# Opening of w_in turned tile by tile, expert choice by rank, and constant products at the last experts

## The chip, the cores and the metric

The kernel runs on one core of a Trainium2 chip. Its engines run side by side, each through its own list of instructions: TensorE (PE in the profile, PEld its weight loads), VectorE (DVE), ScalarE (ACT), GpSimd (POOL), and SyncE (SP), which issues most of the transfers. They wait for each other by semaphores. The metric is the time of the core on the device, in microseconds, as the median of several executions.

## The reference

Two transformer blocks over 256 tokens with 1024 features, in float32. What matters here:

- The first block begins with `rms_norm(x, attn_norm_g) @ w_in` (1024 to 2496 columns), from which latent attention and retention are computed. A cross attention to 256 memory tokens follows.
- Then comes a hierarchical mixture of 32 experts in 4 groups of 8. Each token takes the group with the highest biased logit, and in it the two experts with the highest biased logits; ties go to the lower index:

```python
g_sel = argmax(g_logits + b_group)
g_w = softmax(g_logits)[g_sel]
e_logits = e_all[g_sel]                        # 8 of 32
_, top_idx = top_k(e_logits + b_expert[g_sel], 2)
top_p = softmax(e_logits)[top_idx]; top_p /= sum(top_p)
y = sum over the two of g_w * top_p * (silu(h @ w_gate[e]) * (h @ w_up[e])) @ w_down[e]
```

- The second block (its own projection `w_fin`, feed-forward networks, a recurrent part) is touched only where a helper that it shares has a new signature.

## The kernel before

The 256 tokens are two tiles `t` of 128 rows. Weights arrive in parts of 1 MB or less in a ring of slots; SyncE issues them in one order, and waits before each until the slot's last user on TensorE is done.

The opening. `start_sp` loads the identity, the two halves of `x` under one semaphore `x_in`, and the gain rows; ScalarE and VectorE begin with a wait for both halves (L2931, L2939). For each tile `norm_act` squares and sums on ScalarE (L418), GpSimd takes the power -0.5 (L429, L430), ScalarE scales (L424). TensorE turns the tile in eight transposes (`norm_pe`, L445). VectorE multiplies by the gain (L455) and splits the result into a rounded part and a rest (L526, L527). Each part of `w_in` is split too: ScalarE rounds it (`part_high_act`, L507), VectorE forms the rest (`part_low_dve`, L516). `rounded_linear` then makes each chunk of 512 columns for one tile from 24 products (L482 to L484: high by high, high by low, low by high, for 8 row blocks). A chunk has two parts of the weight. For `w_in` it turned both tiles first and then went chunk 0 and 1 for tile 0, chunk 0 and 1 for tile 1, then chunk by chunk. ScalarE copies tile 0's chunks (L819), VectorE tile 1's (L825). For `w_fin` it gave TensorE some constant products first and turned the second tile after the first chunk.

The routing (`moe_pe`, `moe_dve`, `moe_act`). TensorE makes the 36 logits per tile (L1372). While VectorE picks, TensorE makes seven constant products of the identity (`keep_running`, L466), whose result nobody reads. VectorE picks the group by maximum and tie rule (`pick`, L1547 to L1551), collects the group's logits and biases tile by tile, and picks twice among 8 experts. Then it signals `experts_picked`. TensorE ranks the tokens of each expert by products with a triangle and with ones (L1379 to L1384), VectorE turns the ranks into selection matrices (L1581, L1589), TensorE gathers the tokens (L1395), and from there each of eight quads of experts goes through gate and up products (`gu_quad_pe`, L1344), a transpose (L1235), down products (`down_quad_pe`, L1359) and a scatter product (L1416) that VectorE adds to `X` (L1629). ScalarE's four exponentials (L1507, L1510) give the gate values. The experts' weights go through 17 slots; the first reuse of a slot waits for the semaphore `gate_half`, which the first quad's gate products set.

Of the kernel before, what the change touches and what calls it, by code (L numbers as in the profile page):

```python
# [10 lines left out]
ALU = mybir.AluOpType  # L11
# [118 lines left out]
def build(nc, out, phases="ABCDEFGO", **A):  # L130
    ctx = ExitStack()
    with ctx:
# [442 lines left out]
        def start_sp(sp):  # L575
            sp.dma_start(const[:, 0:P], A["const_table"][:, 0:P]).then_inc(sem("ident_in"), 16)
            sp.dma_start(X[:, 0], A["x"][0, 0:P]).then_inc(sem("x_in"), 16)
            sp.dma_start(X[:, 1], A["x"][0, P:S]).then_inc(sem("x_in"), 16)
# [9 lines left out]
        def small_sp(sp):  # L588
# [4 lines left out]
            for i, name in enumerate(("hy_q_gain_2", "hy_k_gain_2")):  # L593
                for half in range(2):
                    sp.dma_start(cols[half * HD:(half + 1) * HD, P + i:P + i + 1],
                                 A[name][0].unsqueeze(1)).then_inc(sem("gain2_in"), 16)
            sp.dma_start(gain_c, A["moe_norm_g"][0].rearrange("(p k) -> p k", k=KD)).then_inc(sem("gain_c_in"), 16)
# [101 lines left out]
        def mixA_pe(pe):  # L699
            rounded_linear(pe, "a", "w_in", "AD", True)  # L700
# [474 lines left out]
        def cross_dve(dve):  # L1175
# [28 lines left out]
            dve.wait_ge(sem("gain_c_in"), 16)  # L1204
# [107 lines left out]
        flags = rtv(384, 1, rt=rt2).bitcast(I32)  # L1312
        if "C" in phases:
# [49 lines left out]
        def moe_pe(pe):  # L1363
# [11 lines left out]
            keep_running(pe, 7)  # L1375
# [158 lines left out]
        def moe_dve(dve):  # L1534
            L = links["dve"]
            V = nc.vector
            for t in range(T):
# [1440 lines left out]
```

## Time and profile before

| | us |
|---|---|
| median of three runs | 1316.61 (1313.44 to 1319.57) |
| profiled execution | 1314.14, span 1312.3 |
| busy: TensorE products | 1189.7 (91%) |
| busy: VectorE | 737.0 (56%) |
| busy: ScalarE | 247.2 (19%) |
| moved by transfers | 247.27 MB, mean 188 GB/s |

A busy share is an average over stages with different limits. The chain that ended last, and the windows of a stage, tell which engine or transfer sets the length there. Products are pipelined, so a busy TensorE isn't TensorE at its peak. A float32 product of 512 columns is two records in the trace, a transpose is one, and each of the three rounded products is one.

### The profile page before, as it was taken

The page shows a single profiled execution, that of the slowest core. Times are in us where ns is not written, and L with a number is a line of the kernel's source. Part 1 is how long each engine was busy: PE and PEld are TensorE (multiplying, and loading weights), DVE is VectorE, ACT ScalarE, POOL GpSimd, SP SyncE. Part 2 cuts the span into 40 slices and gives each one's busy share as a digit, 9 for nine tenths or more (in the row PEclk, how much of TensorE's full clock was granted, in tenths as well). Part 3 has the DMA queues.
Part 4 walks back from the last instruction along what each step waited for, and adds up shares of the span by engine and source line. Part 5 has one row for each costly group of instructions (what it writes and reads, how often), then busy time and mean ns, then how long its engine had stood idle before and what let it go on. Part 6 is the DMA issues. An engine that isn't in the chain of part 4 may idle for free.

```text
span 1312.3 us, 20905 instructions
## 1 busy us (share of the span) xinstructions
PE 1189.7 (91%) x9007; PEld 862.5 (66%) x9007; DVE 737.0 (56%) x1191; ACT 247.2 (19%) x427; POOL 92.3 (7%) x86
## 2 busy tenths in 40 slices
PE   5999999899876668999999999899999879999997
PEld 4855644556433333996588888667689774788886
DVE  5547421223221112665777877676965647877774
ACT  5413212121000002433100000344222010100000
POOL 2010000010000000120000000000300531000000
PEclk9999999899988889999999999998999999999999
DMA  9653135085999999533855550345100307655600
GB/s 347 199 192 128 65 129 216 40 336 231 419 421 414 422 421 399 190 137 101 284 187 176 183 193 0 97 143 194 40 3 3 111 24 257 226 190 193 190 3 32
DMA packets 106499, 247.27 MB, mean 188 GB/s; under 512 B 7121, under 2 KB 61408, under 8 KB 93986
## 3 DMA queue, kind: packets, MB, share of 16 engines
q1 hardware_dynamic: 106212, 245.71, 51.2%
q8 instruction: 74, 1.21, 0.4%
q0 software_dynamic: 144, 0.15, 0.0%
q14 instruction: 23, 0.19, 0.0%
q10 hardware_dynamic: 46, 0.01, 0.0%
HBM read 244.80 MB, written 1.05 MB: 187 GB/s over the span
## 4 chain that ended last, share of the span: by engine, by line
PE 81%; DMA 9%; DVE 4%; SPq 2%; ACT 2%; issue 1%; POOL 0%; DVEq 0%
PE bank L483 14%; PE bank L482 14%; PE bank L484 14%; PE bank L345 8%; PE bank L331 6%; DMA work<-expert_w_gate 5%; PE bank L2421 4%; PE bank L1344 3%; DMA work<-expert_w_down 2%; PE bank L1359 2%; SPq L301 2%; DMA ring_w<-expert_w_gate 1%; PE bank L1395 1%; PE bank L2315 1%; PE bank L466 1%
## 5 line engine op out<-in xcount | busy, mean ns | idle before, releaser
L482 PE MATMUL bank<-work_rounded,work_rounded 128*128 128x512 f32 (+2 forms) x704 | 276.7, 393 | 6.8 <-DVE work_rounded L1718 5.2
L484 PE MATMUL bank<-work_rounded,work_rounded 128*128 128x512 f32 (+2 forms) x704 | 273.1, 388 | 0.0
L483 PE MATMUL bank<-ring_w_rounded,work_rounded 128*128 128x512 f32 (+2 forms) x576 | 225.8, 392 | 0.0
L482 PEld LDWEIGHTS bank<-work_rounded,work_rounded 128*128 128x128 f32 x704 | 132.8, 189 | 34.4 <-issue 3.9
L484 PEld LDWEIGHTS bank<-work_rounded,work_rounded 128*128 128x128 f32 x704 | 132.3, 188 | 25.3
L483 PEld LDWEIGHTS bank<-ring_w_rounded,work_rounded 128*128 128x128 f32 x576 | 109.4, 190 | 20.3 <-issue 0.2
L345 PE MATMUL bank<-ring_w,work 128*128 128x512 f32 x256 | 112.1, 594 | 3.1 <-ACT work L1149 1.4
L1718 DVE TENSOR_TENSOR ring_w_rounded<-ring_w,work_rounded 128x1024 fp32r<-128x1024 f32 x84 | 102.9, 1225 | 2.9
L1242 ACT ACTIVATE work<-bank 128x256 f32<-128x256 f32 x52 | 20.1, 386 | 426.0 <-PE bank L484 340.3
L345 PEld LDWEIGHTS bank<-ring_w,work 128*128 128x128 f32 x256 | 47.8, 190 | 60.7 <-issue 56.6
L331 PE MATMUL bank<-ring_w,work 128*128 128x512 f32 x192 | 83.5, 593 | 0.9 <-DVE work L455 0.9
L1344 PE MATMUL bank<-ring_w,work 128*32 128x256 f32 x512 | 51.9, 429 | 34.6 <-DMA ring_w<-expert_w_gate 16.2
L1622 DVE TENSOR_TENSOR work<-bank,cols 128x512 f32<-128x512 f32 x16 | 11.1, 691 | 113.8 <-PE bank L1395 113.7
L483 PE MATMUL bank<-work_rounded,work_rounded 128*128 128x512 f32 x192 | 74.9, 390 | 0.0
L331 PEld LDWEIGHTS bank<-ring_w,work 128*128 128x128 f32 x192 | 36.2, 190 | 45.2 <-issue 44.0
L1718 DVE TENSOR_TENSOR work_rounded<-work,work_rounded 128x1024 fp32r<-128x1024 f32 (+1 forms) x56 | 64.3, 1149 | 1.9
L1344 PEld LDWEIGHTS bank<-ring_w,work 128*32 128x32 f32 x512 | 26.7, 123 | 52.5 <-issue 46.3
L1717 DVE CAST work_rounded<-bank 128x256 fp32r<-128x256 f32 x44 | 18.6, 424 | 75.3 <-PE bank L1784 75.3
L1717 DVE CAST work_rounded<-ring_w 128x1024 fp32r<-128x1024 f32 x84 | 57.4, 684 | 0.0
L429 POOL TENSOR_SCALAR stat<-stat 128x1 f32<-128x1 f32 (+3 forms) x21 | 7.5, 356 | 705.1 <-ACT work L418 603.0
L819 ACT COPY work<-bank 128x512 f32<-128x512 f32 (+3 forms) x53 | 28.0, 561 | 124.0 <-PE bank L331 57.3
L1344 PE MATMUL bank<-work 128*32 128x256 f32 x384 | 38.7, 440 | 13.3 <-DMA work<-expert_w_gate 13.3
(446 smaller groups left out, 1821.5 us busy)
## 6 DMA issues: line engine op xcount, KB each, us to landing
ring_w<-ffn_w_down SPq DMA_DIRECT2D x22, 1024.0 KB, 5.1
ring_w<-expert_w_gate SPq DMA_DIRECT2D x16, 1024.0 KB, 17.1
ring_w<-expert_w_up SPq DMA_DIRECT2D x16, 1024.0 KB, 21.9
work<-expert_w_down SPq DMA_DIRECT2D x16, 1024.0 KB, 26.9
work<-expert_w_up SPq DMA_DIRECT2D x13, 1024.0 KB, 21.7
ring_w<-expert_w_down SPq DMA_DIRECT2D x12, 1024.0 KB, 26.0
work<-ffn_w_gate SPq DMA_DIRECT2D x12, 1024.0 KB, 5.4
work<-ffn_w_up SPq DMA_DIRECT2D x12, 1024.0 KB, 8.0
```

Of the source, the lines that this page charges most:

```text
L301: sp.dma_start(unit_view(name) if dst is None else dst, src).then_inc(arrived[slots[0]], 16)
L331: mm = nc.tensor.matmul(ps[:, 0:w_], lhsT[:, kk, t * P:(t + 1) * P], wv[kk // step][:, kk % step, :], start=kk == 0, stop=kk == kt - 1)
L345: mm = nc.tensor.matmul(ps[:, :], lhsT[:, k, t * P:(t + 1) * P], wv[k // 4][:, k % 4, :], start=k == 0, stop=k == KD - 1)
L482: nc.tensor.matmul(out, lhsT[0], rhs[0], start=first, stop=False)
L483: nc.tensor.matmul(out, lhsT[0], rhs[1], start=False, stop=False)
L484: return nc.tensor.matmul(out, lhsT[1], rhs[0], start=False, stop=last)
L819: nc.scalar.copy(dst, ps[:, 0:dst.shape[1]] if len(dst.shape) == 2 else ps[:, 0:dst.shape[1] * dst.shape[2]].rearrange("p (a b) -> p a b", ...
L1344: mm = nc.tensor.matmul(ps[own, i * FF:(i + 1) * FF], hg[:, q % 2, k, own], units_[j][:, k, :], start=k == 0, stop=k == KD - 1)
L1359: mm = nc.tensor.matmul(banks[c][own, :], actT[:, q % 2, k, own], wd[j][:, k, c * 512:(c + 1) * 512], start=k == 0, stop=k == 1)
L1717: links["dve"](nc.vector.tensor_copy(high, value))
L1718: return nc.vector.tensor_tensor(low, value, high.bitcast(F32), ALU.subtract).then_inc(done, 1)
L2421: mm = nc.tensor.matmul(ps[w, h * HD:(h + 1) * HD], lhs(w, 8 * half + h), rhs(w, 8 * half + h), start=True, stop=True)
```

## The change

- Opening: each half of `x` has its own semaphore. ScalarE waits for the half that it needs, VectorE for neither. ScalarE rounds the weight parts 0 and 1 between the two tiles (before: part 0 alone). TensorE turns tile 0, makes nine constant products 128 columns wide, makes chunk 0 for tile 0, then turns tile 1, and goes on with chunk 0 for tile 1, and chunk 1 for both. VectorE splits tile 1 ahead of the weight parts 2 and 3.
- Routing: the biases are added where the logits are copied. The own group's biased logits are collected for both tiles at once. An expert is picked if fewer than two of the eight are ahead of it, where "ahead" is a larger value, or an equal value and a lower index. What the pick doesn't need (negated maxima, raw logits of the group) comes after the signal `experts_picked`. The constant products before the ranking are three instead of seven.
- Last experts: three constant products between the last quad's transposes and its down products, into the quad's gate and up bank.
- The gains' two semaphores are one. `w_fin` keeps its order: its constant products and first turn are moved to its caller.

```diff
-        def keep_running(pe, n):
+        def keep_running(pe, n, bank=BANK[7], width=512):
             for _ in range(n):
-                nc.tensor.matmul(BANK[7][:, :], ident, const[:, 0:512], start=True, stop=True)
+                nc.tensor.matmul(bank[:, 0:width], ident, const[:, 0:width], start=True, stop=True)
...
-        def rounded_linear(pe, u, name, rings, both_first, ahead_of={}):
-            starts = range(parts_of(name)[-1][0] + 1)
-            if not both_first:
-                keep_running(pe, 2)
-            norm_pe(pe, u, tiles=range(T) if both_first else (0,))
-            if not both_first:
-                keep_running(pe, 3)
-            for c, t in [(0, 0), (1, 0), (0, 1), (1, 1)] + [(c, t) for c in starts[2:] for t in range(T)]:
-                if (c, t) == (1, 0) and not both_first:
+        def rounded_linear(pe, u, name, rings, order, ahead_of={}):
+            rest = range(2, parts_of(name)[-1][0] + 1)
+            for c, t in order + [(c, t) for c in rest for t in range(T)]:
+                if (c, t) == order[1]:
                     norm_pe(pe, u, tiles=(1,))
...
-            rounded_linear(pe, "a", "w_in", "AD", True)
+            norm_pe(pe, "a", tiles=(0,))
+            keep_running(pe, 9, width=P)
+            rounded_linear(pe, "a", "w_in", "AD", [(0, 0), (0, 1), (1, 0), (1, 1)])
...
-            norm_act(act, "a", X, ready=lambda t: part_high_act(act, "w_in", 0) if t else None)
-            for n in range(1, 4):
+            def ready(t):
+                if t:
+                    part_high_act(act, "w_in", 0)
+                    part_high_act(act, "w_in", 1)
+                act.wait_ge(sem(f"x{t}_in"), 16)
+            norm_act(act, "a", X, ready=ready)
+            for n in (2, 3):
                 part_high_act(act, "w_in", n)
...
+            norm_split_dve(dve, "a", "attn_norm_g", 1)
             part_low_dve(dve, "w_in", 2)
             part_low_dve(dve, "w_in", 3)
-            norm_split_dve(dve, "a", "attn_norm_g", 1)
...
-            keep_running(pe, 7)
+            keep_running(pe, 3)
             pe.wait_ge(sem("experts_picked"), 1)
...
                 tr_pe(pe, "moe", q, pick=lambda k: slice(k, FF, 2))
+                if q == NQ - 1:
+                    keep_running(pe, 3, RINGS["GU"][q % 2])
                 down_quad_pe(pe, q)
...
+                if t == 0:
+                    dve.wait_ge(sem("const2_in"), 16)
+                    L(V.tensor_scalar(tieinv, tie, -1.0, 8.0, ALU.mult, ALU.add))
+                    L(V.tensor_tensor(earlier, bc(tie, EPG, 2), bc(tie, EPG, 1), ALU.is_gt))
+                    L(V.tensor_scalar(slot_key, C("iota")[:, 0:CAP], -FAR, None, ALU.add))
                 ps = take(dve, "D", f"logit.{t}")
+                V.tensor_tensor(gb[:, t], ps[:, 0:G], bias_g, ALU.add)
+                V.tensor_tensor(biased[:, t], ps[:, G:36], bias_e, ALU.add)
                 V.tensor_copy(logit[:, t], ps[:, 0:36]).then_inc(moved["D"], 1)
...
+            own_group = bc(oh, EPG, 3)
+            L(V.tensor_tensor(tmp, by_group(biased), own_group, ALU.mult))
+            L(V.reduce_sum(bias8, tmp.rearrange("p t g e -> p t e g"), AX.X))
+            mine, other = bc(bias8, EPG, 3), bc(bias8, EPG, 2)
+            L(V.tensor_tensor(ahead[:, :, :, EPG:], other, mine, ALU.is_equal))
+            V.tensor_tensor(ahead[:, :, :, 0:EPG], other, mine, ALU.is_gt)
+            L(V.tensor_tensor(ahead[:, :, :, EPG:], ahead[:, :, :, EPG:], bc(earlier, T, 1), ALU.mult))
+            L(V.reduce_sum(oh2, ahead, AX.X))
+            for t in range(T):
+                last = V.scalar_tensor_tensor(picked[:, t].rearrange("p (g e) -> p g e", g=G), bc(oh2[:, t], G, 1), 2.0,
+                                              bc(oh[:, t], EPG, 2), ALU.is_lt, ALU.mult)
             last.then_inc(sem("experts_picked"), 1)
+            V.tensor_scalar(oh1, oh2, 2.0, None, ALU.is_lt)
+            V.tensor_reduce(nm[:, :, 0], logit[:, :, 0:G], AX.X, ALU.max, negate=True).then_inc(sem("negmax"), 1)
+            L(V.tensor_tensor(tmp, by_group(logit[:, :, G:]), own_group, ALU.mult))
+            L(V.reduce_sum(el, tmp.rearrange("p t g e -> p t e g"), AX.X))
+            V.tensor_reduce(nm[:, :, 1], el, AX.X, ALU.max, negate=True).then_inc(sem("negmax"), 1)
...
-            act.wait_ge(sem("x_in"), 16 * T)
...
-            dve.wait_ge(sem("x_in"), 16 * T)
```

## Rows read from the trace of the kernel before

**Rows 1.** The page's chain that ended last, shares of the span by engine.
```profile
PE 81%; DMA 9%; DVE 4%; SPq 2%; ACT 2%; issue 1%; POOL 0%; DVEq 0%
```

**Rows 2.** Timeline of TensorE, opening and before the routing: start us, us, engine, line, operation [idle before].
```profile
8.65 0.45 PE L614 MATMUL bank<-const,work 127*128 127x127 f32 x1 [8.65 <-DMA work<-rw_mu]
10.32 1.97 PE L445 MATMUL bank<-const,work 128*128 128x128 f32 x8 [1.23 <-ACT work L424]
17.34 1.97 PE L445 MATMUL bank<-const,work 128*128 128x128 f32 x8 [5.05 <-ACT work L424]
...
286.90 1.09 PE L445 MATMUL bank<-const,work 128*128 128x128 f32 x8 [0.60 <-ACT work L424]
```

**Rows 3.** Stretch of `w_in`: length, busy (instructions) PE, PEld, DVE, ACT, POOL; clock, DMA share, GB/s.
```profile
19.30:74.10 54.80, 54.80 (x244) 45.54 (x243) 30.86 (x46) 24.35 (x29) 4.54 (x8) 1.00 0.72 253
```

**Rows 4.** Timeline of VectorE, routing.
```profile
291.73 0.20 DVE L1541 COPY work<-bank 128x36 f32<-128x36 f32 x1 [2.85 <-PE bank L1372]
...
298.48 0.29 DVE L1573 TENSOR_TENSOR work<-work 128x32 f32<-128x32 f32 x2
...
301.31 0.76 DVE L1589 TENSOR_TENSOR work<-work 128x256 f32<-128x256 f32 x2
...
307.34 0.23 DVE L1640 TENSOR_TENSOR work<-work 128x64 f32<-128x64 f32 x1
```

**Rows 5.** Timeline of TensorE, ranking and gather.
```profile
300.19 0.30 PE L1379 MATMUL bank<-work,const 128*128 128x32 f32 x2
...
301.88 3.81 PE L1395 MATMUL bank<-work 128*128 128x128 f32 x32 [0.49 <-DVE work L1589]
```

**Rows 6.** Stretches of the constant products alone (PE, PEld), then clock, DMA share, GB/s.
```profile
291.50:296.75 5.25, 5.25 (x6) 2.16 (x7) 0.50 1.00 415
296.75:300.15 3.40, 3.40 (x9) 1.33 (x7) 1.00 0.05 19
```

**Rows 7.** Stretch of the experts, columns as in rows 3.
```profile
310.20:521.20 211.00, 156.99 (x1536) 84.29 (x1536) 41.48 (x74) 18.07 (x35) 0.00 (x0) 0.89 1.01 414
```

**Rows 8.** Timeline of SyncE's queue, where the stream goes on.
```profile
310.23 0.80 SPq L301 DMA_DIRECT2D const<-expert_w_up  x2
```

**Rows 9.** Timeline of ScalarE, opening.
```profile
7.01 1.06 ACT L418 ACTIVATE work<-X 128x1024 f32<-128x1024 f32 x1 [3.15 <-DMA X<-x]
...
9.12 1.15 ACT L424 ACTIVATE work<-X,stat 128x1024 f32<-128x1024 f32 x1 [0.96 <-POOL stat L430]
10.47 1.90 ACT L507 CAST work_rounded<-ring_w 128x2048 fp32r<-128x2048 f32 x1 [0.20 <-DMA ring_w<-w_in]
...
16.14 1.15 ACT L424 ACTIVATE work<-X,stat 128x1024 f32<-128x1024 f32 x1 [2.72 <-POOL stat L430]
```

**Rows 10.** Timeline of SyncE's queue, opening.
```profile
1.19 0.42 SPq L577 DMA_DIRECT2D X<-x  x1
...
5.04 2.42 SPq L301 DMA_DIRECT2D ring_w<-w_in  x4
```

**Rows 11.** Landing of `x` after its issue, and of the part of `w_in` issued at 5.48.
```profile
DMA to landing us min/median/max: 3.8/4.6/5.3
...
ring_w<-w_in SPq DMA_DIRECT2D x1, 1024.0 KB, 7.6
```

**Rows 12.** Timeline of VectorE, opening.
```profile
11.54 0.69 DVE L455 TENSOR_TENSOR work<-bank,cols 128x512 f32<-128x512 f32 x1 [2.05 <-PE bank L445]
...
13.34 2.35 DVE L516 TENSOR_TENSOR ring_w_rounded<-ring_w,work_rounded 128x1024 fp32r<-128x1024 f32 x2
...
36.49 0.69 DVE L825 COPY work<-bank 128x512 f32<-128x512 f32 x1 [2.76 <-PE bank L484]
...
74.06 0.62 DVE L825 COPY work<-bank 128x448 f32<-128x448 f32 x1 [9.15 <-PE bank L484]
```

**Rows 13.** Chain of waits in order of time, first quad's gate products.
```profile
306.52 3.66 PE bank L1344 x64
```

**Rows 14.** Timeline of TensorE, last down products.
```profile
513.72 3.64 PE L1359 MATMUL bank<-work 128*32 128x512 f32 x32 [2.23 <-DMA work<-expert_w_down]
```

More of the change, by code:

```diff
@@ L1312, in build @@
         flags = rtv(384, 1, rt=rt2).bitcast(I32)
+        biased = rtv(0, T, NE, rt=rt2)
+        ahead = rt2[:, 64:320].rearrange("p (t e x) -> p t e x", t=T, e=EPG)
+        earlier = rtv(400, EPG, EPG, rt=rt2)
+        tieinv = rtv(400, 8)
         if "C" in phases:
@@ L1536, in moe_dve @@
             V = nc.vector
+            tie = C("gidx")
+            FAR = 1024.0
             for t in range(T):
@@ L1541, in moe_dve @@
+                V.tensor_tensor(biased[:, t], ps[:, G:36], bias_e, ALU.add)
                 V.tensor_copy(logit[:, t], ps[:, 0:36]).then_inc(moved["D"], 1)
             await_moved(dve, "logit.1")
-            tie = C("gidx")
-            def pick(dst, v, m, n):
-                L(V.tensor_reduce(m[:, :, 0], v, AX.X, ALU.max))
-                L(V.tensor_tensor(tmp8[:, :, 0:n], v, bc(m[:, :, 0], n, 2), ALU.is_equal))
-                L(V.tensor_tensor(dst, tmp8[:, :, 0:n], bc(tieinv[:, 0:n], T, 1), ALU.mult))
-                L(V.tensor_reduce(m[:, :, 0], dst, AX.X, ALU.max))
-                L(V.tensor_tensor(dst, dst, bc(m[:, :, 0], n, 2), ALU.is_equal))
@@ L1553, in moe_dve @@
-            tieinv = rtv(400, 8)
-            dve.wait_ge(sem("const2_in"), 16)
-            L(V.tensor_scalar(tieinv, tie, -1.0, 8.0, ALU.mult, ALU.add))
-            L(V.tensor_reduce(nm[:, :, 0], logit[:, :, 0:G], AX.X, ALU.max))
-            V.tensor_scalar(nm[:, :, 0], nm[:, :, 0], -1.0, None, ALU.mult).then_inc(sem("negmax"), 1)
-            L(V.tensor_tensor(gb, logit[:, :, 0:G], bc(bias_g, T, 1), ALU.add))
-            pick(oh, gb, m1, G)
-            for t in range(T):
-                L(V.tensor_tensor(tmp[:, t], logit[:, t, G:].rearrange("p (g e) -> p g e", g=G), bc(oh[:, t], EPG, 2), ALU.mult))
-                L(V.reduce_sum(el[:, t], tmp[:, t].rearrange("p g e -> p e g"), AX.X))
-                L(V.tensor_tensor(tmp[:, t], bias_e.rearrange("p (g e) -> p g e", g=G), bc(oh[:, t], EPG, 2), ALU.mult))
-                L(V.reduce_sum(bias8[:, t], tmp[:, t].rearrange("p g e -> p e g"), AX.X))
@@ L1565, in moe_dve @@
-            L(V.tensor_reduce(nm[:, :, 1], el, AX.X, ALU.max))
-            V.tensor_scalar(nm[:, :, 1], nm[:, :, 1], -1.0, None, ALU.mult).then_inc(sem("negmax"), 1)
-            L(V.tensor_tensor(bias8, bias8, el, ALU.add))
-            pick(oh1, bias8, m1, EPG)
-            L(V.scalar_tensor_tensor(bias8, oh1, -3e38, bias8, ALU.mult, ALU.add))
-            pick(oh2, bias8, m1, EPG)
-            L(V.tensor_tensor(oh1, oh1, oh2, ALU.add))
-            for t in range(T):
-                last = V.tensor_tensor(picked[:, t].rearrange("p (g e) -> p g e", g=G), bc(oh[:, t], EPG, 2),
-                                       bc(oh1[:, t], G, 1), ALU.mult)
@@ L1575, in moe_dve @@
-            last.then_inc(sem("experts_picked"), 1)
-            FAR = 1024.0
-            L(V.tensor_scalar(slot_key, C("iota")[:, 0:CAP], -FAR, None, ALU.add))
+            L(V.tensor_reduce(m1[:, :, 0], gb, AX.X, ALU.max))
+            L(V.tensor_tensor(tmp8[:, :, 0:G], gb, bc(m1[:, :, 0], G, 2), ALU.is_equal))
+            L(V.tensor_tensor(oh, tmp8[:, :, 0:G], bc(tieinv[:, 0:G], T, 1), ALU.mult))
+            L(V.tensor_reduce(m1[:, :, 0], oh, AX.X, ALU.max))
+            L(V.tensor_tensor(oh, oh, bc(m1[:, :, 0], G, 2), ALU.is_equal))
@@ L1901, in fox_pe @@
         def fox_pe(pe):
+            keep_running(pe, 2)
+            norm_pe(pe, "d", tiles=(0,))
+            keep_running(pe, 3)
             def turn_qk():
@@ L2091, in turned_qk @@
                 dve.wait_ge(sem("zeros"), 4)
-                dve.wait_ge(sem("gain2_in"), 64)
+                dve.wait_ge(sem("gains_in"), 80)
                 for t in range(T):
```

12 lines of the change are left out of this document (6 added, 6 removed).

## Prediction

> **What bounds the kernel now.** I read the page's chain first: TensorE holds 81% of it and the transfers 9% [rows 1]. So a change pays only where it shortens TensorE's own waits, or where a transfer that ends late starts earlier. Next the timelines of the two places that the change touches, and the table of stretches. In the opening TensorE has almost nothing to do until 17.34 us, when it turns the second tile; the products of `w_in` follow at about 19.3 us [rows 2]. From 19.3 to 74.1 us it is busy without a gap (54.80 of 54.80 us) [rows 3]: the stage is TensorE's own length behind its late start. In the routing VectorE picks the experts until 298.77 us [rows 4], but the ranking products start only at 300.19 us [rows 5]: 14 records of constant products stand ahead of them, 6 of which ran at half clock [rows 6]. After it the experts' weights are the bound: from 310.2 to 521.2 us the transfers are at share 1.01, 414 GB/s, without a pause [rows 7]. That stream had stopped by 297 us for want of free slots (share 0.05 from there [rows 6]) and goes on at 310.23 us, when the first quad's gate products are done [rows 8].
>
> **Opening.** The chain of the first tile starts with the square at 7.01 us, for which both halves of `x` had to land [rows 9]. The first half lands 3.8 us after its issue at 1.19, at 5.0 [rows 10, 11]. From the square's start to the end of the scaled tile is 9.12 + 1.15 - 7.01 = 3.26 us [rows 9], so that tile is ready at 8.3 instead of 10.27. The transpose of the gain rows, ahead on TensorE, is at 8.65 [rows 2], so the eight transposes go at about 9.0. VectorE starts 1.22 us behind them (11.54 - 10.32 [rows 2, 12]), at 10.2. One half tile (product, rounding, rest) takes it 13.34 - 11.54 = 1.80 us, one weight part 2.35 us [rows 12]. The first weight part's rounding on ScalarE ends at 10.47 + 1.90 = 12.37 us as before; it waits for its landing [rows 9]. So on VectorE: half 0 to 12.0; part 0 from 12.37 to 14.7; half 1 to 16.5; part 1 to 18.85, its first half at 17.7. Part 1 lands at 5.5 + 7.6 = 13.1 us [rows 10, 11], and ScalarE, which now rounds it ahead of tile 1's square, has it at 15.0, ahead of VectorE's need at 16.5.
>
> A chunk of one tile takes TensorE 5.55 us (three of them between 19.3 and 36.45, with about 0.5 us more in the slow start [rows 2, 12]). The second half of chunk 0 starts at 17.7 and ends at 20.5. Tile 1 meanwhile: ScalarE squares it from 15.0 to 16.15, GpSimd's power takes 2.72 us from the square to the scaling, as it did beside a busy VectorE [rows 9], scaling ends at 20.0, just ahead of need. Transposes from 20.5; VectorE from 21.1; half 0 ready at 22.9. TensorE loses this wait, which is the price of turning tile by tile: some 1.4 us between transposes and products. Chunk 0 of tile 1 then runs from 22.9 to 28.45 (the second half of tile 1's features is ready at 24.7, needed at 25.7). Parts 2 and 3 follow on VectorE to 27.0 and 29.4; needed at 28.45 and 31.2. Later parts keep their lead: ScalarE copies chunk 1 at 34 to 34.6 us, rounds parts 4 and 5 to 38.4, and they are first needed at 39.5 (second halves at 42.3), while VectorE is through with its rotary angles by 34. Before, two chunks were done by 36.45 - 5.55 = 30.9, so the rest of the stage is 74.02 - 30.9 = 43.1 us of products, so it ends at 71.55 instead of 74.02. I take 2.4 us gained. The nine small products sit between 11 and 15 us, where TensorE is idle, and cost nothing while they end ahead of 14.7; even twice as long they delay only the first half of chunk 0, which has until 17.7.
>
> Bounds of this term: 2.9 gained if the handover from tile 1's transposes to its products takes 0.4 us less than I put. At the other end, the transposes at 17.34 took 1.97 us for eight, those at 286.90 took 1.09 [rows 2]: early products run at half rate (1.2 of 2.4 GHz; the granted clock in the table says 1.00 there, the durations say otherwise). If the second half of chunk 0 ran so, it costs 2.8 us more: 0.4 lost. A page bears on this. The Trainium skill, "TensorE: Matmul & The Clock Gate", Part 4 (PE-mode transpose), says that transposes do not count as activity towards the full clock in the way that products do. By it the nine products, not the eight transposes, would raise the clock here; no row of before separates the two.
>
> **Routing.** Instructions on VectorE from the logits (291.73) to the pick (298.77): 7.04 us, 34 small ones, most of them linked, 0.20 us from one start to the next on the mean (7.04 / 34 = 0.21) [rows 4]. New: two additions more that read the logits from PSUM, side by side, +0.26, so linked work starts at 292.2. Then five small linked (group maximum, tie, own group), 5 x 0.20: 293.2. Product and sum over groups, 64 elements a partition, 2 x 0.27 by the 0.23 us row: 293.7. `is_equal`, `is_gt` and the tie mask on 128 elements: between 0.23 us (64) and 0.38 us (256, two in 0.76) [rows 4], I take 0.32, 0.25 and 0.32: 294.6. Sum over 16: 0.42: 295.05. Two fused products: 0.29: 295.35. So the pick is 3.4 us earlier. Should the four-dimensional forms cost twice, it is at 296.6.
>
> TensorE: the fill starts at 291.50. At half clock six records took 5.25 us [rows 6]; three products are six records, so the fill ends at 296.75, later than the pick either way. Ranking starts at 296.8 instead of 300.19: 3.4 us gained. If the clock is high all through, six records take 6 x 0.43 = 2.6 us (3.40 us for the last eight [rows 6]), the fill ends at 294.1, and the pick decides: 4.8 us gained. If the clock stays low after the short fill, ranking (0.86 us), gather (3.81) and the first gate products (3.66) [rows 5, 13] take twice as long, 8.3 us more: 4.8 lost.
>
> What was taken out of the pick (the flags, both negated maxima, the own group's raw logits) is five instructions, 1.1 us, done at 296.5 under the ranking products, whose result comes at 297.7. ScalarE's four exponentials then end at about 297.4, and VectorE asks for them 1.2 us after the ranking result. The three constant preparations at the first logits fill part of the 1 us in which VectorE waited for them. The merged semaphore costs nothing: its transfers land by 40 us and are asked for at 270.
>
> From the ranking's start to the restart of the stream is 310.23 - 300.19 = 10.04 us [rows 5, 8], untouched. So the restart is at 310.23 - 2.4 - 3.4 = 304.4. The stream's length is set by bytes at share 1.01 [rows 7], so its end moves as much.
>
> **Last experts.** TensorE has 2.23 us of idle time before the last down products, whose weights come at 513.7 [rows 14]. Six records at full clock take 2.6 us: it starts 0.35 us late. At half clock it would be 2.9 us late; if without the fill another execution fell to half clock there, the fill saves up to the 3.64 us of those products [rows 14]. I take 0.35 lost.
>
> **Sum.** 2.4 + 3.4 - 0.35 = 5.45 us. The profiled execution took 1314.14 us (span 1312.3): 1308.7. It lies 2.5 us under the median of its runs, so for the median 1316.61 - 5.45 = 1311.2.
>
> **Rivals.**
> The clock stays high in the routing: VectorE decides, and the gain there is 4.8. Against it: the profile shows the drop, after a stretch of transposes and of products only 36 wide. For it: the profile shows the drop in one execution, and nothing says that it comes in each. Total 6.85 gained: 1309.8.
> The opening is not passed on: tile 1 comes late, or early products run slow. For it: three engines meet within 0.5 us at 20 us. Against it: the first tile's work is plainly 1 us earlier. Routing and last experts alone: 3.05 gained: 1313.6.
> The other side, slower: with four fill products fewer TensorE idles before the ranking and stays at 1.2 GHz up to the restart of the stream, on the one path where that counts. Price 8.3 us: 2.4 + 3.4 - 8.3 - 0.35 = 2.85 lost: 1319.5. It decides from 5.45 us of chain work at the low clock. Against it: in the profile the clock came back at 296.75, when the new fill would end, and all of TensorE's work up to there is kept.
> The Trainium skill, "TensorE: Matmul & The Clock Gate", the part on HAM oscillation, says that TensorE which idles between bursts is throttled again and begins each burst cold. It speaks for this rival; the trace agrees that the clock falls (0.50 from 291.50 to 296.75).
> The gains do not reach the end, because the experts' stream is late for another reason: 0.35 lost, 1317.0. The unbroken share of 1.01 speaks against it.
>
> **Numbers.** Forecast 0.50, clock high 0.20, opening lost 0.15, slower 0.10, not passed on 0.05. A measurement here tells 0.5% (6.6 us) from no change; three runs of before spread over 6 us. Faster by more than that is below 1310.0: some 0.4 of the forecast's share, half of the first rival's, 0.05 of the rest: 0.35. Slower is above 1323.2: 0.04, since even the slow rival ends at 1319.5 and needs the runs' spread on top; 0.61 remain. Range 1306.0 to 1317.0.
>
> **What would show it.** In the profile after: the square on ScalarE near 5 us; the first product of `w_in` by 15 and the stage's last copy on VectorE near 71.6; a gap of about 1.4 us between tile 1's transposes and products; from the second logits to the ranking 5 us instead of 8.5; the stream's restart 5.8 us earlier, at share 1.0 until 5.8 us earlier than before; the last down products right behind three constant ones. It is wrong if the ranking is at half clock past its start, if the stage up to 74 us has a second gap, or if the stream pauses.

## The result, and the profile after

The changed kernel takes 1301.5 us (median of 4 runs, 1296.6 to 1304.1), the kernel before 1315.4 beside it: ratio 0.9886, 95% interval 0.9847 to 0.9924. Forecast were 1311.2 us and a gain of 5.45; the gain is some 14 us in this pair, and the time lies below the range. Three later comparisons, each on a chip of its own, gave 0.9900, 0.9901 and 0.9886, with gains of 11.6, 12.4 and 13.4 us between the means. So the direction was right and the size was not. Two of the executions timed beside e9 to e12 took 2429 and 5610 us and are left out of every mean.

The profiled execution took 1304.06 us (span 1302.0), 10.1 us less than the one of before (10.3 in the spans). Where they went, read from marks that both traces have; the last row, the tail, is all that comes behind the experts:

| stretch | before, us | after, us | difference |
|---|---|---|---|
| start to the last copy of `w_in` | 74.06 | 72.75 | -1.3 |
| to the last addition of `w_co` to X | 207.92 | 211.24 | +3.3 |
| to the ranking's first product | 18.21 | 12.56 | -5.6 |
| to the stream's restart | 10.04 | 10.07 | 0.0 |
| to the last quad's first down product | 203.49 | 202.51 | -1.0 |
| to the last addition of the experts | 7.50 | 7.50 | 0.0 |
| to the end of the span (the tail) | 791.1 | 785.4 | -5.7 |

The change touches nothing in rows two and seven, and yet the tail is the largest term. One pair of executions does not say what belongs to the kernel; the experiments do.

First the touched places, TensorE's timeline of the changed kernel, which answers to [rows 2, 5, 14] (start us, us, engine, line, operation, idle before; `...` marks lines left out):

```profile
9.40 1.91 PE L445 MATMUL bank<-const,work 128*128 128x128 f32 x8
11.11 3.76 PE L466 MATMUL bank<-const 128*128 128x128 f32 x18
14.62 0.48 PE L482 MATMUL bank<-work_rounded,work_rounded 128*128 128x512 f32 x1
...
18.23 0.50 PE L482 MATMUL bank<-work_rounded,work_rounded 128*128 128x512 f32 x1 [0.57 <-DVE ring_w_rounded L516]
...
21.14 1.04 PE L445 MATMUL bank<-const,work 128*128 128x128 f32 x8
23.80 0.47 PE L482 MATMUL bank<-work_rounded,work_rounded 128*128 128x512 f32 x1 [1.63 <-DVE work_rounded L527]
...
292.74 2.82 PE L466 MATMUL bank<-const 128*128 128x512 f32 x6
296.55 0.41 PE L1385 MATMUL bank<-work,const 128*128 128x32 f32 x2 [0.98 <-DVE work L1577]
...
298.27 3.81 PE L1401 MATMUL bank<-work 128*128 128x128 f32 x32 [0.42 <-DVE work L1597]
...
506.46 2.74 PE L466 MATMUL bank<-const 128*128 128x512 f32 x6
509.13 3.64 PE L1365 MATMUL bank<-work 128*32 128x512 f32 x32
```

The first product stands at 14.62, and two waits are left where tile by tile was to have one: 0.57 us for the first part's second half and 1.63 us between tile 1's transposes and its products. In the routing the constant products are through at 295.56 and TensorE waits 0.98 us for the pick. The restart of the stream is at 306.62, where 304.4 was forecast: the untouched row two took 3.3 us more. VectorE's side of it, which answers to [rows 4, 12], and the queue's and ScalarE's rows, which answer to [rows 8, 9]:

```profile
72.75 0.62 DVE L822 COPY work<-bank 128x448 f32<-128x448 f32 x1 [9.15 <-PE bank L484]
...
292.95 0.16 DVE L1556 TENSOR_TENSOR work<-bank,rowsmall 128x4 f32<-128x4 f32 x1 [2.07 <-PE bank L1378]
...
294.89 0.29 DVE L1572 TENSOR_TENSOR work<-work 128x128 f32<-128x128 f32 x1
295.22 0.29 DVE L1573 TENSOR_TENSOR work<-work 128x128 f32<-128x128 f32 x1
295.43 0.28 DVE L1574 TENSOR_TENSOR work<-work 128x128 f32<-128x128 f32 x1
295.74 0.42 DVE L1575 TENSOR_REDUCE work<-work 128x16 f32<-128x256 f32 x1
296.20 0.29 DVE L1577 SCALAR_TENSOR_TENSOR work<-work 128x32 f32<-128x32 f32 x2
...
306.62 0.80 SPq L301 DMA_DIRECT2D const<-expert_w_up  x2
```
```profile
5.30 1.06 ACT L418 ACTIVATE work<-X 128x1024 f32<-128x1024 f32 x1 [1.45 <-DMA X<-x]
...
10.96 1.90 ACT L507 CAST work_rounded<-ring_w 128x2048 fp32r<-128x2048 f32 x1 [2.40 <-DMA ring_w<-w_in]
```

From the first read of the last logits to the end of the pick are 3.54 us (292.95 to 296.49) where there were 7.04. Stretches of the changed kernel, for [rows 3, 6, 7] (length, busy PE, PEld, DVE, ACT, POOL; clock, DMA share, GB/s):

```profile
19.30:72.75 53.45, 51.82 (x235) 43.08 (x234) 28.58 (x44) 25.04 (x30) 5.26 (x7) 1.00 0.73 261
...
292.74:295.56 2.82, 2.82 (x8) 1.04 (x7) 2.30 (x13) 0.00 (x0) 0.00 (x0) 1.00 1.01 421
...
306.62:516.63 210.01, 161.68 (x1542) 85.55 (x1542) 41.47 (x74) 18.07 (x35) 0.00 (x0) 0.88 1.01 415
```

The stream is as full as before (share 1.01). The three constant products ran at the full clock here, in an execution in which they were to have run at half.

### The profile page after: what moved, and what is told of

Same layout as the page of the kernel before. It is cut to its first block, busy times and chain, and to the rows that moved or that the text cites. A ratio compares the mean times of both kernels' runs of the same rounds, so it can differ in the third digit from the quotient of the medians.

```text
span 1302.0 us, 20925 instructions
## 1 busy us (share of the span) xinstructions
PE 1187.7 (91%) x9023; PEld 859.9 (66%) x9023; DVE 735.8 (57%) x1181; ACT 247.0 (19%) x427; POOL 92.3 (7%) x86
## 3 DMA queue, kind: packets, MB, share of 16 engines
q8 instruction: 74, 1.21, 0.4%
## 4 chain that ended last, share of the span: by engine, by line
PE 76%; DVE 10%; DMA 9%; ACT 2%; SPq 2%; issue 1%; POOL 0%; DVEq 0%
PE bank L483 13%; PE bank L482 13%; PE bank L484 13%; PE bank L345 9%; PE bank L331 6%; DMA work<-expert_w_gate 5%; PE bank L2432 4%; PE bank L1350 4%; DMA ring_w<-expert_w_gate 3%; PE bank L1365 2%; SPq L301 1%; DVE ring_w_rounded L2278 1%; PE bank L1401 1%; PE bank L1088 1%; PE bank L1792 1%
## 5 line engine op out<-in xcount | busy, mean ns | idle before, releaser
L1350 PE MATMUL bank<-ring_w,work 128*32 128x256 f32 x512 | 53.4, 442 | 33.0 <-DMA ring_w<-expert_w_gate 17.1
L1042 DVE TENSOR_TENSOR X<-X,bank 128x512 f32<-128x512 f32 x12 | 8.2, 687 | 75.5 <-PE bank L345 75.5
```

Source lines behind the costliest of these rows:

```text
L1350: mm = nc.tensor.matmul(ps[own, i * FF:(i + 1) * FF], hg[:, q % 2, k, own], units_[j][:, k, :], start=k == 0, stop=k == KD - 1)
```

## The experiments

Eighteen kernels ran, each beside the kernel before; e1 to e4, e5 to e8, e9 to e12, e13 to e16, and e17 with e18 each share a chip. Differences are of the means, with one standard error; the clock is the mean granted clock over the executions. A half-clock spell is a stretch in which TensorE was granted half of its clock.

| run | against before, us | clock, this / before |
|---|---|---|
| e1 opening only | -6.3 +- 1.3 | 0.9708 / 0.9689 |
| e2 routing only | -2.5 +- 1.0 | 0.9697 / 0.9689 |
| e3 last experts only | -6.0 +- 1.3 | 0.9736 / 0.9689 |
| e4 changed kernel | -11.6 +- 1.5 | 0.9725 / 0.9689 |
| e5, e6 before with 3, 9 tiny products | -0.6 +- 1.0, -1.0 +- 1.1 | 0.9703, 0.9708 / 0.9699 |
| e7 changed with 56 tiny products | -7.3 +- 1.3 | 0.9726 / 0.9699 |
| e8 changed, 3 tiny, no last products | -6.6 +- 1.4 | 0.9696 / 0.9699 |
| e9 changed kernel | -12.4 +- 1.7 | 0.9740 / 0.9699 |
| e10 opening only | -3.8 +- 1.2 | 0.9692 / 0.9699 |
| e11, e12 changed, before: recurrent stage filled | -8.1, +4.4 +- 1.0 | 0.9729, 0.9684 / 0.9699 |
| e13, e14 before, 1, 2 products later | +1.3 +- 1.1, -0.2 +- 1.2 | 0.9702, 0.9722 / 0.9710 |
| e15 changed, 2 products later | -1.2 +- 0.8 | 0.9680 / 0.9710 |
| e16 changed, no last products | -6.5 +- 1.3 | 0.9709 / 0.9710 |
| e17 changed, 4 products later | -7.4 +- 1.4 | 0.9737 / 0.9714 |
| e18 changed kernel | -13.4 +- 1.7 | 0.9766 / 0.9714 |

**The change in parts.** Each of the first three takes only its part of the change.

```diff
 e1: everything in start_sp, mixA_*, rounded_linear, fox_pe
 e2: moe_dve, and keep_running(pe, 7) -> keep_running(pe, 3)
 e3: + if q == NQ - 1: keep_running(pe, 3, RINGS["GU"][q % 2])
```

> Kernel before with the opening alone changed (own waits for the halves of x, turned tile by tile, nine small constant products, VectorE's and ScalarE's new order); routing and last experts as before. Theory 1 (each touched place gives what its own stage shows, the rest of the 14 us is the clock of TensorE in stages the change does not touch, and comes and goes from execution to execution): w_in's last copy on VectorE at 72.7 instead of 74.1 us, gain 1.3 to 2.4 us, so 1313 to 1314; the stages after 521 us may differ by 5 us either way between single profiles, but follow their time at half clock. Theory 2 (the change has a lasting effect on the later stages, by the shift of the opening): 5 us or more gained, about 1309, with less time at half clock after 520 us.

> Kernel before with the routing alone changed (choice by rank, three constant products instead of seven); opening and last experts as before. Theory 1: second logits to ranking 3.6 us instead of 8.5, the experts' stream restarts 4.9 to 5.6 us earlier, all of it arrives at the end: 1309.5 to 1310.5. Rival (the prediction's forecast, fill at half clock in most executions): 3.4 us gained, 1312. Theory 2: routing gives more than its stage shows, 8 us or more, through later stages.

> Kernel before with three constant products between the last quad's transposes and its down products, nothing else. Theory 1: 0.35 us lost to 1 us gained, no difference that can be measured, about 1315. Theory 2b (without the fill TensorE falls to half clock behind the last quad in many executions, and the fill keeps the scatter, the next opening and what follows at full clock): 3 to 6 us gained, 1309 to 1312, and the time at half clock after 505 us falls.

> The changed kernel once more, beside the three parts on the same chip. Theory 1: the sum of the three parts within 3 us, 1303 to 1308, since the 14 us of the first measurement held some 5 us of luck with the clock; the stage after the last down products agrees with the kernel before's to 0.5 us once half of its time at half clock is taken off. Theory 2: 1301 again, and more than the sum of the three parts.

Routing alone gave 2.5 us: near the forecast's 3.4, and half of what theory 1 put. The other two gave more than their stages. The last products, for which I had put a loss, gave 6 us. The three parts add up to 14.9 +- 2.1 us, the whole (e4) gave 11.6 +- 1.5, so the parts are no clean shares. A part of the reason is plain in the trace. TensorE with the last down products waiting, first in e2, without the constant products, then in e16, which has none either:

```profile
503.37 0.39 PE L1235 MATMUL bank<-const,work 128*128 128x128 f32 x2
505.80 5.34 PE L1363 MATMUL bank<-work 128*32 128x512 f32 x32 [2.04 <-DMA work<-expert_w_down]
```
```profile
502.19 3.64 PE L1365 MATMUL bank<-work 128*32 128x512 f32 x32 [1.93 <-DMA work<-expert_w_down]
```

The granted clock falls in the wait or up to 0.5 us behind it, and the same 32 products take 5.34 instead of 3.64 us. Of the 11 profiled kernels without the constant products 9 show this (waits of 2.0 to 3.7 us, products of 5.0 to 6.4 us), the kernel before and e16 do not; the 9 with them never do (7.50 us from the first of these down products to the last addition). Over the 11 the loss is 1.4 us on the mean. The fill's own cost shows ahead of the products: from the stream's restart to the first of them are 202.0 to 202.5 us in seven of the nine kernels with the fill and 201.7 to 201.9 in eight of the eleven without; the other five lie at 202.9 to 203.7. So the fill costs 0.4 us, as predicted, and saves 1.4: the stage explains 1.0 of the 6 us.

**Does the length of the instruction stream matter?** My first theory for the rest was that the tail's waits for instructions depend on how many instructions stand ahead of it.

```diff
 e5: + if q in (5,): keep_running(pe, 3, RINGS["GU"][(q + 1) % 2], width=8)
 e6: the same with 9
 e7: the changed kernel + the same with 14 for q in (2, 3, 5, 6)
 e8: the changed kernel, - the last products, + the line of e5
```

> Kernel before with three products 8 columns wide (12 entries in TensorE's instruction stream, as many as the last fill has) in the wait for the experts' weights of quad 5, where TensorE idles some 7 us. They cost nothing there. Theory A (blocks of TensorE's instructions: the recurrent stage from 840 to 1090 us loses 1 to 2 us at each of some numbers 256 apart in TensorE's stream, and a shift of the stream moves these against the waits): as e3_last_only but for the last quad's 1.7 us, so 4 to 6 us gained, 1310 to 1312, and the time from the last addition of the experts' stage to the end is 787 us instead of 791. Theory B (TensorE's clock alone, which comes and goes from execution to execution): no change, 1315 to 1316.

> The same with nine tiny products (36 entries, the shift that the opening alone makes). Theory A: as e1_opening_only but for the opening's own 2.4 us: 4 to 6 us gained, 1310 to 1312; the stalls at entries 13153 and 13409 sum to less than the 3.4 us of before. Theory B: no change, 1315 to 1316.

> The changed kernel with 56 tiny products (224 entries) in the waits of quads 2, 3, 5 and 6, so that with its own 32 the recurrent stage stands as in the kernel before against blocks of 256. They should cost nothing in those waits. Theory A: 4 to 6 us slower than the changed kernel, 1308 to 1310, and the last stages take 789 to 791 us instead of 785. Theory B: no change, 1303 to 1304.

> The changed kernel without the three products at the last experts, and three tiny ones (the same 12 entries) in quad 5's wait instead: only the last fill's own effect is gone, its place in the instruction stream is kept. Theory A: 1 to 2 us slower than the changed kernel, 1305 to 1306, since in most executions the last down products and scatter then run 3.4 us at half clock (9.2 us from them to the last addition instead of 7.5). Rival (the fill itself, not the instruction count, gives e3 its 7 us, through the clock in later stages): 6 to 7 us slower, 1310.

On the kernel before nothing came of it: the tiny products move the numbers of all later instructions, and e5 and e6 gained 0.6 and 1.0 us where the theory had 4 to 6. e8 speaks against it too: 5.9 us less gained than by the changed kernel on the mean of e4, e9 and e18 (12.5), where the theory had 1 to 2 less. e7 does not: 5.2 us less gained and a tail of 791.4 us are what the theory forecast. So the theory failed in three of four runs and is not refuted by e7, and the changed kernel itself did not run on that chip.

**The rest goes with the clock.** Over the 336 executions timed with the experiments, within a kernel, the time falls by 0.93 us for each 0.001 of mean granted clock (correlation -0.81). Brought to one clock, the changed kernel is 8.3, 8.6 and 8.6 us faster than before in its three jobs (e4, e9, e18). The other 3.4 to 4.8 us come with a clock higher by 0.0036 to 0.0052. That is a correlation, and it takes out what the last products save by the clock as well. By the same sum opening only is 4.5 and 4.4 us faster (e1, e10), routing 1.8, the last products 1.6, e7 4.7 and e8 6.8. Repeated on another chip, with two edits against half-clock spells in the recurrent stage beside it:

```diff
-            keep_running(pe, 4)
+            keep_running(pe, 6)
 and the 32 products of 4 columns ("fraw") four behind each feature block of w_rv's first chunk
```

> The changed kernel again, on another chip. So far its total fell 12 to 14 us below that of the kernel before, while the stages that the change touches are shorter by some 7.5 us in the profiles (opening 2.3, routing 3.5, last experts 1.7). Theory S: only the touched stages count, and the rest was the mix of clock spells in stages that the change leaves alone: 6.5 to 8.5 us faster here. Rival K: the change does something more in every execution that the marks of the touched stages miss: 12 to 14 us faster again.

> The kernel before with the opening turned by tile, on another chip. Its stage is shorter by 2.3 us in the profiles, its total was 6.3 us lower on the first chip (8 against the median of before). Theory S: 2 to 3 us faster here. Rival K: 6 to 8 us faster again.

> The changed kernel with two edits in the recurrent stage, which the change does not touch: six constant products in place of four before the first products of w_rk (TensorE waits about 2.1 us there), and the 32 products of 4 columns, so far in one row (3.96 us), laid four after each feature block of w_rv's first chunk. In the profiles a half-clock spell begins at or right behind each of these two places in most executions and makes 8 to 16 wide products 0.43 us long in place of 0.23. If such spells are what moves the total in untouched stages: 2 to 4 us faster than the changed kernel of this job, and no spell near 837 and 905 us. If they are hidden or come from elsewhere: no difference, within 1 us.

> The kernel before with the same two edits in the recurrent stage and nothing of the change. Theory S: 2 to 4 us faster than the kernel before, as the changed kernel gains by them. Rival K, in which the change itself had cured the spells behind it (the changed kernel's first profile had none after 503 us): here the gain is larger than on the changed kernel, 5 us or more, and the difference between the two kernels shrinks to about 7 us.

The changed kernel repeated (K, on the total), opening only came between the two. The filled stage lost 4 us on both, not gained. The trace of the changed kernel and that of e11 tell the two edits apart, both at full clock in these stretches:

```profile
831.11 1.06 PE L445 MATMUL bank<-const,work 128*128 128x128 f32 x8 [1.60 <-ACT work L424]
837.75 0.47 PE L482 MATMUL bank<-ring_w_rounded,work_rounded 128*128 128x512 f32 x1 [2.14 <-DVE work_rounded L2665]
...
912.35 0.40 PE L482 MATMUL bank<-ring_w_rounded,work_rounded 128*128 128x512 f32 x1
```
```profile
831.27 1.06 PE L445 MATMUL bank<-const,work 128*128 128x128 f32 x8 [1.63 <-ACT work L424]
837.90 0.48 PE L482 MATMUL bank<-ring_w_rounded,work_rounded 128*128 128x512 f32 x1 [0.42 <-DVE work_rounded L2669]
...
906.15 0.48 PE L482 MATMUL bank<-ring_w_rounded,work_rounded 128*128 128x512 f32 x1 [2.66 <-issue]
...
915.29 0.48 PE L482 MATMUL bank<-ring_w_rounded,work_rounded 128*128 128x512 f32 x1
```

The two constant products more lie in the wait and cost nothing: the first product stands 6.6 us behind the transposes in both. The narrow products cost 2.8 us: in one row they had covered a wait, spread over the products they leave TensorE idle for 2.66 us, and the 25th of these products comes at 915.29 instead of 912.35, in a kernel that was 0.16 us late. In e12 the clock falls 1 us behind that newly opened wait, for 17.1 us. No spell follows the filled wait in the profiles of e11 and e12, where that of the kernel before has one of 3.4 us at 842.9 (that of the changed kernel has none there either, without the fill). So most of the 4 us is the second edit's own cost; whether the first alone would gain was not run.

What differs between the kernels in the tail is seen best in stretches that begin at equal distances behind the last addition of the experts (columns as above). The kernel before, the changed kernel, and the changed kernel with two products more at the start of the tail (e15, so that each of its stretches covers work that lies 1.7 us earlier in the program):

```profile
837.22:851.22 14.00, 11.86 (x43) 8.23 (x43) 13.07 (x20) 5.99 (x5) 0.92 (x3) 0.88 0.18 43
...
906.22:916.22 10.00, 10.00 (x46) 7.89 (x45) 5.11 (x10) 7.50 (x9) 0.00 (x0) 0.75 0.57 211
916.22:931.22 15.00, 15.00 (x62) 12.06 (x61) 14.66 (x16) 1.57 (x3) 5.08 (x2) 0.94 0.21 69
```
```profile
832.63:846.63 14.00, 11.86 (x50) 8.22 (x50) 13.82 (x22) 6.00 (x5) 0.90 (x3) 1.00 0.22 43
...
901.63:911.63 10.00, 10.00 (x57) 8.12 (x57) 5.11 (x9) 7.12 (x9) 0.00 (x0) 1.00 0.55 208
911.63:926.63 15.00, 15.00 (x66) 12.07 (x65) 14.66 (x16) 1.76 (x3) 5.07 (x2) 1.00 0.27 87
```
```profile
833.77:847.77 14.00, 11.68 (x51) 8.17 (x52) 13.01 (x20) 7.11 (x7) 1.34 (x4) 1.00 0.34 72
...
902.77:912.77 10.00, 10.00 (x50) 7.48 (x50) 5.10 (x11) 6.72 (x9) 0.00 (x0) 0.90 0.64 210
912.77:927.77 15.00, 15.00 (x63) 12.01 (x62) 14.69 (x15) 2.36 (x3) 5.07 (x2) 0.95 0.27 87
```

In the second stretch TensorE is busy 10.00 of 10.00 us in all three, but 57 records fit into it at the clock 1.00 and 46 at 0.75. The products behind the 32 narrow ones show it singly, in the kernel before and in the changed one:

```profile
908.67 4.56 PE L2345 MATMUL bank<-const,work 128*128 128x4 f32 x32
913.09 0.77 PE L482 MATMUL bank<-ring_w_rounded,work_rounded 128*128 128x512 f32 x1
913.66 0.63 PE L483 MATMUL bank<-ring_w_rounded,work_rounded 128*128 128x512 f32 x1
```
```profile
903.18 3.63 PE L2356 MATMUL bank<-const,work 128*128 128x4 f32 x32
906.67 0.48 PE L482 MATMUL bank<-ring_w_rounded,work_rounded 128*128 128x512 f32 x1
906.98 0.39 PE L483 MATMUL bank<-ring_w_rounded,work_rounded 128*128 128x512 f32 x1
```

Fourteen profiled kernels have the same instructions in the tail. All four profiles of the changed kernel had no half-clock spell in it before its last microseconds and took 784.8 to 786.1 us (mean 785.4). The other ten had 6.8 to 23.9 us of spells and took 786.3 to 795.7 (mean 790.3); e7 is one of them, with 13.7 us of spells and 791.4. The correlation of tail and half-clock time is 0.93; a straight fit gives 0.36 us for each us at half clock and 0.54 for each us that TensorE waited with "issue" as the cause.

**Why has the changed kernel none?** The program in the tail is the same, so my theory was that the moment decides at which its waits meet the clock. This was put to the test by moving that moment; the edit adds products on TensorE's path to do it.

```diff
             norm_pe(pe, "d", tiles=(0,))
-            keep_running(pe, 3)
+            keep_running(pe, 4)
```

That is e13 (on the kernel before the lines stand in `rounded_linear`); e14 and e15 have 5 there, e17 has 7. e16 is the changed kernel without the line of e3, e18 the changed kernel.

> The kernel before with one more constant product (two records, 0.86 us at full clock) ahead of the first products of w_fin at 527 us, on TensorE's path: everything behind it comes 0.9 us later. Theory M (the moment decides how many half-clock spells the recurrent stage meets; in the profiles the tail behind the last addition to X takes 785 to 786 us where it begins as in the changed kernel, 791 where it begins some 1.7 us later): a shift by 0.9 us changes the tail by something between nothing and -5 us, total -4 to +1. Rival D (the products at the last experts act directly, the moment does nothing): 0.9 us slower, the same clock.

> The kernel before with two more such products, 1.7 us later from 527 us on. Theory M: this is the largest shift away from where its tail begins now, so the tail shrinks by 4 to 5 us and the kernel is 2 to 4 us faster than before although it does more, at a mean granted clock higher by 0.003. Rival D: 1.7 us slower, the same clock.

> The changed kernel with the same two more products behind the experts. Theory M: its tail then begins where that of the kernels without the last products does, and is 4 to 5 us longer, so it is 5 to 7 us slower than the changed kernel, which leaves 6 to 8 us against the kernel before, at a clock lower by 0.003. Rival D: 1.7 us slower, 10 to 11 us faster than the kernel before.

> The changed kernel without the three constant products at the last experts, all else kept. The stages touched give 5.8 us against the kernel before (opening 2.3, routing 3.5). Theory M: the last experts end 1.7 us later, and the tail is 4 to 5 us longer: 5 to 7 us faster than the kernel before, so 5 to 6 us slower than the changed kernel. Rival D says nearly the same of this run, and it alone does not tell them apart. If neither holds: 1.7 us slower than the changed kernel, 10 to 11 faster than before.

> The changed kernel with four more constant products ahead of the first products of w_fin, 3.4 us later from 523 us on. That is the length of the shortest half-clock spell in the profiles; the others are whole multiples of it. Theory M: a shift of this size meets the spells as the changed kernel itself does, so only the 3.4 us are lost: 3 to 4 us slower than the changed kernel of this job, at the same mean clock, and faster than with two products (8 to 9 us faster than the kernel before, where two gave 1). Rival W (work put on the path costs a multiple of its length, wherever it ends): slower than with two, so not faster than the kernel before.

> The changed kernel beside it. Theory M: 11 to 14 us faster than the kernel before, mean granted clock about 0.973 against 0.970. If the extra is a matter of the chip: 6.5 to 8.5 us faster at a clock of 0.970, and the loss of the run with two products was then 6 us, not 11.

Two products, 1.7 us, took 11 us from the changed kernel (e15, -1.2, against -12.5 on the mean of e4, e9 and e18; it did not run beside e15). That is 5 us more than theory M put, which had 6 to 8 us of gain left, and 9 more than D. Four products, 3.4 us, took only 6 (e17 against e18, 6.0 +- 2.0) and left it 6.2 +- 1.6 faster than with two. More work on the path, less time: neither a direct effect of the last products (D) nor a price on added work (W) gives that. M does in direction, though e17 too lost more than the 3 to 4 us that it put. The clock says the same, 0.9680 with two products against a kernel before at 0.9710, 0.9737 with four against 0.9714. In the profile of e17 these stretches are at full clock again (a spell of 6.8 us follows only at 1027 us), and its tail less the added 3.4 us is 786.0 us:

```profile
896.91:906.91 10.00, 10.00 (x55) 7.51 (x54) 6.06 (x10) 5.64 (x10) 0.00 (x0) 1.00 0.56 209
906.91:921.91 15.00, 15.00 (x66) 12.09 (x65) 13.60 (x14) 4.18 (x4) 4.92 (x2) 1.00 0.27 87
```

e16 shows the last products' share at 6 us, as e3 did: 1.0 in their stage; that the rest comes from ending the stage earlier is argued, not shown. On the kernel before a shift did less than theory M put: two products cost nothing (-0.2 +- 1.2 instead of +1.7), but the 2 to 4 us of gain did not come, and one product cost what D put (1.3 +- 1.1 against 0.9). No version beat the changed kernel.

## Why the prediction was wrong

**Opening, right in the gain, by some luck.** Forecast 2.4 us. The last copy of `w_in` stands at 72.3 to 72.9 us in the profiles of eleven kernels with the new opening and at 72.1 in a twelfth, at 74.1 to 75.8 in eight with the old one: 2.5 us on the mean. The single pair shows 1.3, since the profile of before is the earliest of its eight. The forecast end of the stage, 71.6, was 1.0 us early against the mean of the twelve, 72.6; that the gain came out as put is due to the old opening, which takes 75.0 us on the mean and not the 74.1 of its one profile. The pieces came close: square at 5.30 (4.97 put), first product at 14.62 (by 15), handover 1.63 us (1.4). Not foreseen was that the first part lands half a microsecond later (rounded from 10.96 instead of 10.47), which gives the 0.57 us wait; so tile 1's transposes start at 21.14 (20.5 put) and its products at 23.80 (22.9 put), and that lateness stays to the end. These eight transposes took 1.04 us, at full clock. The Trainium skill, "TensorE: Matmul & The Clock Gate", Part 4 (PE-mode transpose), would have products and not transposes raise the clock; the order of the rows agrees (1.91 us for eight at 9.40, ahead of the constant products, and 1.04 behind), but it does not separate the two, as no kernel left the constant products out.

**Routing, right; in the profile of after by another path.** Forecast 3.4 us, with the constant products as the limit. From the last addition of `w_co` to the ranking the kernels with the old routing take 16.05 us (18.2 where a half-clock spell lies at 290), those with the new one 12.57 (14.7 with the spell): 3.5 us less in either. The rival "clock stays high" described what the profile shows, VectorE's pick as the limit and 0.98 us of waiting. Its gain of 4.8 us counted from an execution whose own constant products were slow; against one that has them fast it is 3.5. From the last logits to the ranking are 3.6 us in that profile, where 5 had been named as the sign. The forecast's own path occurred in the five of eleven profiles of the new routing that have the spell at 290, here in e4, where the slow constant products run up to the ranking:

```profile
291.39 5.43 PE L466 MATMUL bank<-const 128*128 128x512 f32 x6
296.65 0.31 PE L1385 MATMUL bank<-work,const 128*128 128x32 f32 x2
```

The rival in which the ranking runs at half clock did not occur: from it to the restart are 10.0 to 10.2 us in every profile.

**Last experts, the step that failed.** The prediction took 0.35 us lost, because the constant products are 0.4 us longer than the wait. That cost was right (0.4 us); the saving, put at nothing, was the error. Measured: 1.4 us saved in the stage, so 1.0 gained, and 6 us in the total (e3; e16 against e4, e9, e18). Both sides of it stood in the working: "if without the fill another execution fell to half clock there, the fill saves up to the 3.64 us of those products". I chose by the one execution that I had, and that was one of the two among eleven in which the clock held. The Trainium skill, the same page, the part on HAM oscillation, says that an engine that waits long between bursts begins the next one cold; I weighed it for the routing, where it spoke against the change, and not here, where it speaks for it. The profiles agree in nine of eleven, with waits of 2.0 to 3.7 us.

**The sum, the second failure.** It let what lies behind the experts come through one for one. With the stages as measured it would have been 2.5 + 3.5 + 1.0 = 7.0 us, some 1.5 short of the 8.3 to 8.6 at one clock; e8, without the last products, fits it (6.6 measured, 6.0 from its stages), e7 in the total (7.3) but not at one clock (4.7). The other 4 us go with half-clock spells of stages that nobody touched: the tail of the changed kernel took 785.4 us on the mean of four, that of the kernel before and its two versions with tiny products 789.4 (791.1, 790.8, 786.3). That the start of the tail matters, e15 against e17 supports; it is not shown, for the shifts of the kernel before (e13, e14) did not follow. The other way goes the stretch between `w_in` and `w_co`, 3.3 us longer in the profile of after, also by spells: the changed kernel has 10 to 14 us of them there in all four profiles, the kernel before and its two versions 3 to 7. But e8, e16 and e17, which are the changed kernel up to there, have 3, 0 and 3 us, so these spells differ between executions of the same instructions.

**Open.** Why the kernel before gains little from a shift (e14), why opening alone gave 6.3 and 3.8 us (4.5 and 4.4 at one clock) for a stage of 2.5, and why e4, e9 and e18 repeat the extra 4 us while e7, equal up to tiny products, does not. Each kernel has one profile, and only its mean clock is known of the other executions. What fixes the moment itself was not tried.

## What to carry to other kernels

Where TensorE waits 2 us ahead of products on the path, a few constant products in the wait can be worth more than they overrun it, here 1.4 us against 0.4: judge by what the clock does over several executions, not in the one at hand. Narrow products that lie in a wait are free there and cost time elsewhere (2.8 us in e11). A sum over stages gives what a change does at one clock; more (here some 4 us) can come or go in stages behind it that are only shifted, so time a change again with a shift of a microsecond or two before its parts are believed.

## What the runs showed of the hardware

More added work on TensorE's path can cost less than a little: the changed kernel, 12.5 us faster than the kernel before, was 1.2 +- 0.8 us faster with 1.7 us added (e15) and 7.4 +- 1.4 with 3.4 us added (e17).

In the recurrent stage, where the products are 64 columns wide, TensorE stops for 0.7 to 2.2 us at a time with "issue" as the cause, which is time in which the profile shows nothing awaited. TensorE's timeline of the kernel before:

```profile
1016.13 0.21 PE L2480 MATMUL bank<-ring_w,work 64*64 64x64 f32 x1 [0.70 <-issue]
1019.91 0.74 PE L2421 MATMUL bank<-work 64*64 64x64 f32 x18 [1.52 <-issue]
1025.62 1.74 PE L2421 MATMUL bank<-ring_w,work 64*64 64x64 f32 x53 [1.83 <-issue]
```

These three lie 256 TensorE instructions apart, and three more follow at 1054 to 1074 us. Queue 8, of the page's kind "instruction", moves 16 KB 2.4 to 2.7 us ahead of each of the six (74 packets, 1.21 MB in all on the page). In sum all waits with this cause were 4.6 to 8.8 us of the tail in the kernels with the same instructions there. That the fetch is what TensorE waits for was not tested.
